# GpSimd builds eight of the twenty-four first one-hots that ScalarE built for the gate tables

## The chip, the cores and the metric

The kernel runs on one core of one Trainium2 chip. The metric is the device time of one execution in microseconds (us); lower is better. Times of the profile count from the first instruction of the profiled execution.

## The reference

The program computes one layer of a decoder for 1024 tokens with 1024 channels. It ends in an expert retrieval (PEER): each token has 8 heads, and each head picks 16 of 128 x 128 experts by two sub-keys, with a softmax over the 16 scores as gates.

```python
idx, gates = peer_retrieve(xf, w_query, sub_keys)     # (T, 8, 16) expert numbers and gates
u, v = expert_u[idx], expert_v[idx]                   # 16384 experts of 1024 numbers
act = gelu(einsum('tkd,td->tk', u, x))                # exact gelu
out = einsum('tk,tkd->td', gates * act, v)
```

The rest of the layer (a pooling mixer and a short convolution mixer, two norms, two projections) lies ahead of the part that this change touches.

## The kernel before

**Two ways through the experts.** The 1024 tokens are eight tiles of 128. Four tiles are *gathered*: GpSimd issues one indirect DMA for each of a tile's 128 (head, choice) pairs, for `expert_u` and again for `expert_v` (1024 in all, into a ring of `RING` = 8 slots), and VectorE multiplies or adds each row. The other four tiles are *dense*: TensorE multiplies their tokens with all 16384 experts, and a table of gates, which is zero wherever an expert was not chosen, weights the result.

**The gate tables.** The table of one token is a 128 x 128 matrix, the sum over its 128 choices of (one-hot of the first half of the expert number) times (gate times one-hot of the second half): one matmul with both one-hots as operands. One dense tile is filled by 128 scattering DMAs of GpSimd (`scatter`), the other three (384 tokens) by these matmuls, in `BATCHES` = 48 batches of `HOTS` = 8 tokens. A batch b passes through four engines:

- VectorE makes the gated one-hots of every batch (eight `TENSOR_SCALAR` of 128 x 128, L1467), and for even b the first one-hots too (one `TENSOR_TENSOR`, L1463).
- ScalarE makes the first one-hots of odd b in `first_hots`: eight `Square` activations (L985), a drain, one `Relu` (L987). It does so two batches ahead: in its loop it calls `first_hots(b + 2)` before it evicts batch b.
- TensorE multiplies (L798): eight matmuls, each shown as two in the profile, in two halves that each fill one PSUM bank of four.
- ScalarE evicts each half (L1009, twice a batch) into one of two stages; SyncE writes a stage to HBM after every fourth batch.

The one-hots have `HOTBUFS` = 3 buffers, so a maker of batch b waits until TensorE is done with batch b - 3 (`table_full`). After batches 5, 13, 21, 29, 37 and 45 (`AFTER_BATCH`) TensorE also multiplies one *score tile* of the dense part (L785, eight matmuls of 512 columns), and ScalarE applies Gelu to it (L993). `pe.wait_ge(hot_first, ...)` holds TensorE at odd b until ScalarE's one-hots are there.

**Around it.** Every engine runs its instructions in the order of the code. GpSimd's queue ahead of the tables holds gathers for two tiles' first rows and the 128 scattering DMAs; `rows` = 64 is the number of gathered rows that VectorE uses before the tables, so GpSimd can issue gathers up to number 71 and then waits (`rows_used`) for VectorE, which comes back to rows after the tables. After the tables TensorE runs the dense part (L785 scores, L831 sums) to the end, and its first sums need gate tables that SyncE reads back from HBM (L557) and VectorE multiplies in (L1252).

Of the kernel before, what the change touches and what calls it, by code (L numbers as in the profile page):

```python
# [9 lines left out]
ACT = mybir.ActivationFunctionType  # L10
AX = mybir.AxisListType

P = 128
# [35 lines left out]
RING = 8  # L49
# [3 lines left out]
HOTS = 8  # L53
HOTBUFS = 3
BATCHES = TABLED * P // HOTS
# [30 lines left out]
def program(nc, hT, x_rows, w_all, sub_keys, pool_w, small, rows_g, expert_u, expert_v, uT, out):  # L86
# [57 lines left out]
    with ctx:  # L144
# [3 lines left out]
        def sem(name):  # L148
            return ctx.enter_context(nc.semaphore(name))
# [31 lines left out]
        hots = at(12288, HOTBUFS * 2 * HOTS, KEYS).rearrange("p (c s t) j -> p c s t j", c=HOTBUFS, s=2)  # L181
        tables = at(18432, STAGES * KEYS, CHUNK).rearrange("p (c j) t -> p c j t", c=STAGES)
        routeT = at(26624, 3, TABLED * P)
# [21 lines left out]
        ones = sb("ones", [P, P])  # L205
        iota = sb("iota", [P, KEYS])
# [88 lines left out]
        d_gates = sem("d_gates")  # L295
        turned = sem("turned")
        turned_out = sem("turned_out")
        hot_first = sem("hot_first")
        hot_gated = sem("hot_gated")
        table_full = sem("table_full")  # L300
        table_out = sem("table_out")
# [55 lines left out]
        rows, since_digits = 0, 0.0  # L357
# [118 lines left out]
        for kind, a, b in order:  # L476
# [19 lines left out]
            elif kind == "sum" and a == GROUPS - 1 and b % 2 == 1:  # L496
                beside[x].append(("dense_root", b // 2))

        block = ctx.enter_context(nc.Block())

        @block.sync
# [126 lines left out]
        @block.gpsimd  # L628
        def _(pool):
            pool.wait_ge(const_dve, 1)  # L630
            nc.gpsimd.affine_select(out=ident[:], in_=ident[:], compare_op=ALU.is_equal, fill=0.0, base=0,
                                    pattern=[[-1, P]], channel_multiplier=1).then_inc(const_pool, 1)
            nc.gpsimd.iota(iota[:], [[1, KEYS]], base=0, channel_multiplier=0,
                           allow_small_or_imprecise_dtypes=True).then_inc(const_pool, 1)
            nc.gpsimd.iota(token_u[:, 0:1], [[0, 1]], base=0, channel_multiplier=1).then_inc(const_pool, 1)
            nc.gpsimd.memset(zeros, 0.0).then_inc(zero_ready, 1)

            head_after = [rows_by[1 if h < 3 else 2] + RING - 1 for h in range(HEADS)]

            def scatter(h):
                if h == 0:
                    pool.wait_ge(zeroed, 16 * ZEROED)
                    pool.wait_ge(s_gates, 1)
                else:
                    pool.wait_ge(scattered, 16 * TOPK * h)
                for k in range(h * TOPK, (h + 1) * TOPK):
                    nc.gpsimd.indirect_dma_start(out=g_flat, out_offset=bass.IndirectOffsetOnAxis(ap=place[:, k:k + 1], axis=0),  # L650
                                                 in_=gate[:, k:k + 1], in_offset=None, compute_op=ALU.add).then_inc(scattered, 16)

            def load_xf(t):
                rank = list(GATHERED_RANK)[t]
                pool.wait_ge(kept[rank % GT], 32 * (rank // GT + 1))
                if t >= 2:
                    pool.wait_ge(rows_used, first_row["u", t - 2] + HK)
                pool.dma_start(xf[:, t % 2, :], of_tile(xf_d, GATHERED_TILE[t])).then_inc(xf_in[t % 2], 16)

            for i, (table, t) in enumerate(ROWS):  # L660
                if table == "u":
                    load_xf(t)
                    if t == 2:

                        pool.wait_ge(routed, GATHERED)
                        pool.dma_start(g_final, rows_g[:, D:2 * D]).then_inc(g_final_in, 16)
                    pool.wait_ge(routed, t + 1)
                else:

                    if t == 0:  # L670
                        pool.wait_ge(keyed, 4 * TILES)
                    else:
                        pool.wait_ge(rows_used, first_row["v", t - 1] + 1)
                    pool.dma_start(h2, of_tile(h2_d, GATHERED_TILE[t])).then_inc(h2_in, 16)
                for k in range(HK):
                    r = HK * i + k
                    if r >= RING:
                        pool.wait_ge(rows_used, r - RING + 1)
                    nc.gpsimd.indirect_dma_start(out=ring[:, r % RING, :], out_offset=None, in_=expert_u if table == "u" else expert_v,  # L679
                                                 in_offset=bass.IndirectOffsetOnAxis(ap=idx[:, t, k:k + 1], axis=0)).then_inc(row_in[r % RING], 16)  # L680
                    for h in range(HEADS):
                        if head_after[h] == r:
                            scatter(h)

        @block.tensor
        def _(pe):
# [15 lines left out]
            for s, (kind, n, i) in enumerate(steps):  # L702
# [3 lines left out]
                if kind == "sumsq":  # L706

                    pe.wait_ge(x_added, n + 1)
                    for k in range(2):
                        last = nc.tensor.matmul(pair[:, 0:width(n)], ones[:], sq[:, k, 0:width(n)], start=(k == 0), stop=(k == 1))  # L710
                elif kind == "pa":
                    if i % 2 == 0:
                        w = next_w()
                    for k in range(KD):
                        if i == 0:
                            pe.wait_ge(xn_ready, KD * n + k + 1)
                        last = nc.tensor.matmul(pair[:, 0:width(n)], w[:, k, i % 2 * P:(i % 2 + 1) * P], xnT[n % 2][:, k, 0:width(n)],  # L717
                                                start=(k == 0), stop=(k == KD - 1))
                elif kind == "bcv":
                    w = next_w()  # L720
                    for c in range(2):
                        last = chunk(pair[:, c * 512:c * 512 + width(n)], w, c, xnT[n % 2][:, :, 0:width(n)])
                elif kind == "pool":
                    if n == 0:
                        pe.wait_ge(const_in, 48)
                    for g in range(NG):
                        pe.wait_ge(pooled, n * NG + g + 1)
                        last = nc.tensor.matmul(pair[:, g * GW:(g + 1) * GW], poolw[:, g, :], yT[:, g, :], start=True, stop=True)
                elif kind == "ynorm":

                    pe.wait_ge(y_added, n + 1)
                    for c in range(2):
                        last = nc.tensor.matmul(pair[:, c * GW:(c + 1) * GW], ones[:], sq[:, c * NG, 0:GW], start=True, stop=True)
                elif kind == "outp":
                    half, t = i // GT, i % GT
# [9 lines left out]
                elif kind == "turn":  # L745
                    pe.wait_ge(xf_ready, n * GT + i + 1)
                    for k in range(KD):
                        last = nc.tensor.transpose(pair[:, k * P:(k + 1) * P], xfb[:, i, k * P:(k + 1) * P], ident[:])
# [13 lines left out]
                elif kind == "score":  # L762
                    if i == 0:
                        pe.wait_ge(act_emptied, empty(("query", n, 3)))
                    t, m = i // 2, i % 2
# [23 lines left out]
            for b in range(BATCHES):  # L789
                c = b % HOTBUFS  # L790
                pe.wait_ge(hot_gated, b + 1)
                if b % 2 == 1:
                    pe.wait_ge(hot_first, b // 2 + 1)
                for m in range(2):
                    if 2 * b + m >= 4:
                        pe.wait_ge(table_out, 2 * b + m - 3)
                    for q in range(4):
                        last = nc.tensor.matmul(g_bank[(2 * b + m) % 4][:, q * KEYS:(q + 1) * KEYS], hots[:, c, 0, 4 * m + q, :],  # L798
                                                hots[:, c, 1, 4 * m + q, :], start=True, stop=True)
                    last.then_inc(table_full, 1)  # L800
                if b == ROUTES_AFTER:
                    pe.wait_ge(d_gates, 2)
                    for t in range(1, TABLED):
                        turn_routes(t)
                if b in AFTER_BATCH:
                    x = AFTER_BATCH.index(b)
                    if x == 0:

                        pe.wait_ge(xfT_in, 16)
                        pe.wait_ge(turned_out, TABLED - 1)  # L810
                    score_tile(x)
# [4 lines left out]
            for kind, a, n in dense:  # L816
# [3 lines left out]
                else:  # L820
                    g, t, half = a, n // 2, n % 2
# [14 lines left out]
        def _(act):  # L836
# [143 lines left out]
            def first_hots(b):  # L980
                c = b % HOTBUFS
                if b >= HOTBUFS:
                    act.wait_ge(table_full, 2 * (b - HOTBUFS) + 2)
                for t in range(HOTS):
                    nc.scalar.activation(hots[:, c, 0, t, :], iota[:], ACT.Square, scale=-1.0, bias=routeT[:, 0, b * HOTS + t:b * HOTS + t + 1])  # L985
                act.drain()
                nc.scalar.activation(hots[:, c, 0], hots[:, c, 0], ACT.Relu, scale=-4.0, bias=ones[:, 0:1]).then_inc(hot_first, 1)  # L987

            def gelu_tile(x):
                if x >= GSLOTS:  # L990
# [7 lines left out]
            for b in range(BATCHES):  # L998
                if b - 1 in AFTER_BATCH:
                    gelu_tile(AFTER_BATCH.index(b - 1))  # L1000
                if b % 2 == 1 and b + 2 < BATCHES:
                    first_hots(b + 2)
                for m in range(2):
                    n = 2 * b + m
                    c, q = n // (CHUNK // 4), n % (CHUNK // 4)
                    if q == 0 and c >= STAGES:
                        act.wait_ge(table_kept[c % STAGES], 16 * (c // STAGES))
                    act.wait_ge(table_full, n + 1)
                    nc.scalar.activation(tables[:, c % STAGES, :, 4 * q:4 * q + 4],  # L1009
                                         g_bank[n % 4].rearrange("p (t j) -> p j t", t=4), ACT.Copy).then_inc(table_out, 1)  # L1010
                if b == ROUTES_AFTER:
                    for t in range(1, TABLED):
                        turn_out(t)
                    act.drain()
# [503 lines left out]
```

## Time and profile before

| | |
|---|---|
| time, median of 3 runs | 2557.34 us (2557.06 to 2560.21) |
| the profiled execution: its time | 2559.86 us |
| its span, first to last instruction | 2558.1 us |
| TensorE busy (matmuls) | 2474.3 us, 97% |
| VectorE busy | 1971.3 us, 77% |
| ScalarE busy | 424.1 us, 17% |
| GpSimd busy | 1452.8 us, 57% |

PE is TensorE's matmuls, PEld its weight loads, DVE VectorE, ACT ScalarE, POOL GpSimd, SP SyncE. "Busy" is a share of the whole span and mixes stages with different limits; the table stage lies between 661 and 822 us.

### The profile page before, as it was taken

How to read it: one execution, taken by the hardware profiler on the slowest of the kernel's cores; microseconds unless marked ns; L12 is line 12 of the kernel's file. 1: busy time of each engine (PE TensorE's matmuls, PEld its weight loads, DVE VectorE, ACT ScalarE, POOL GpSimd, SP SyncE). 2: the span in 40 equal slices, each digit the busy share in tenths (PEclk: the TensorE clock that was granted, in tenths of full speed). 3: DMA queues.
4: the chain of work that ended last, by engine and by line, in shares of the span. 5: the costliest groups of instructions: out<-in, count | busy, mean ns of one | idle time of the engine just before them, and what ended most of it. 6: DMA issues, size and time to landing. Idle time of an engine off the chain costs nothing.

```text
span 2558.1 us, 24120 instructions
## 1 busy us (share of the span) xinstructions
PE 2474.3 (97%) x7561; PEld 1360.4 (53%) x7561; DVE 1971.3 (77%) x4252; ACT 424.1 (17%) x782; POOL 1452.8 (57%) x1169
## 2 busy tenths in 40 slices
PE   8999998998888899999999999999999999999998
PEld 7687785867766344444444444444444444444443
DVE  4308879778779788777898778779787877888877
ACT  0213213221887000110010100000000000000001
POOL 0000487677601267666665767667676776766664
PEclk9999999998999999999999999999999999999999
DMA  8544886865666899989999999999999999999997
GB/s 336 214 156 163 315 300 167 347 188 132 198 190 201 333 356 374 396 318 385 388 413 391 383 385 414 394 418 419 419 386 397 412 394 420 419 407 403 420 401 262
DMA packets 288079, 857.68 MB, mean 335 GB/s; under 512 B 42064, under 2 KB 99408, under 8 KB 273360
## 3 DMA queue, kind: packets, MB, share of 16 engines
q0 software_dynamic: 167184, 541.73, 55.4%
q1 hardware_dynamic: 108416, 289.25, 30.0%
q10 hardware_dynamic: 12352, 25.17, 2.6%
q8 instruction: 60, 0.98, 0.1%
q14 instruction: 67, 0.55, 0.1%
HBM read 807.75 MB, written 48.30 MB: 335 GB/s over the span
## 4 chain that ended last, share of the span: by engine, by line
PE 85%; DVE 6%; ACT 4%; DMA 1%; issue 1%; DVEq 1%; POOL 1%; SPq 1%; ACTq 0%
PE pairs L831 34%; PE pairs L785 33%; PE pairs L699 12%; ACT arena L985 2%; PE pairs L742 1%; PE pairs L717 1%; PE pairs L798 1%; ACT arena L1009 1%; DMA arena<-gate_tables 1%; PE pairs L769 1%; ACT pick_all L864 1%; POOL ring L679 1%; DVE topi L1073 0%; DVE topi L1065 0%; ACT arena L987 0%
## 5 line engine op out<-in xcount | busy, mean ns | idle before, releaser
L679 POOL DMA_INDIRECT ring<-in_expert_u,idx x512 | 660.7, 1290 | 610.7 <-DVE dots L1186 343.5
L831 PE MATMUL pairs<-arena 128*128 128x512 f32 x2048 | 883.4, 593 | 7.0 <-DVE arena L1252 6.3
L785 PE MATMUL pairs<-arena 128*128 128x512 f32 x2048 | 882.5, 592 | 0.0
L679 POOL DMA_INDIRECT ring<-in_expert_v,idx x512 | 574.7, 1122 | 290.2 <-DVE arena L1197 129.9
L1186 DVE CUSTOM_DVE_ANT_0 junk<-ring,xf 128x1024 bf16<-128x1024 f32 x512 | 610.5, 1223 | 157.1 <-DMA ring<-in_expert_u,idx 153.0
L831 PEld LDWEIGHTS pairs<-arena 128*128 128x128 f32 x2048 | 389.6, 190 | 498.4 <-issue 497.5
L785 PEld LDWEIGHTS pairs<-arena 128*128 128x128 f32 x2048 | 388.6, 190 | 486.5 <-issue 486.5
L1197 DVE SCALAR_TENSOR_TENSOR arena<-ring,arena 128x1024 f32<-128x1024 f32 x381 | 471.7, 1284 | 63.8 <-DMA ring<-in_expert_v,idx 62.5
L699 PE MATMUL pairs<-arena 128*128 128x256 f32 (+1 forms) x1792 | 399.7, 386 | 7.2 <-ACT arena L946 4.2
L699 PEld LDWEIGHTS pairs<-arena 128*128 128x128 f32 x1792 | 345.5, 193 | 59.5 <-ACT arena L946 5.1
L993 ACT ACTIVATE arena<-pairs 128x512 f32<-128x512 f32 x128 | 76.4, 597 | 1176.2 <-PE pairs L785 1176.2
L650 POOL DMA_INDIRECT gate_tables<-gate,place x128 | 210.8, 1647 | 57.9 <-issue 38.8
L1197 DVE SCALAR_TENSOR_TENSOR xf<-ring,arena,xf 128x1024 f32<-128x1024 f32 x126 | 154.4, 1282 | 8.8 <-DMA ring<-in_expert_v,idx 8.8
L1252 DVE TENSOR_TENSOR arena<-arena 128x512 f32<-128x512 f32 x128 | 87.6, 688 | 61.2 <-ACT arena L993 48.9
L1258 DVE TENSOR_TENSOR arena<-arena,pairs 128x512 f32<-128x512 f32 x128 | 87.5, 684 | 51.6 <-PE pairs L831 50.9
L1467 DVE TENSOR_SCALAR arena<-iota,arena 128x128 f32<-128x128 f32 x384 | 101.3, 347 | 25.5 <-PE pairs L798 25.5
L742 PE MATMUL pairs<-arena 128*128 128x512 f32 x256 | 114.2, 603 | 5.3 <-DVE arena L1377 5.3
L798 PE MATMUL pairs<-arena 128*128 128x128 f32 x768 | 91.4, 277 | 28.1 <-ACT arena L1009 25.3
L798 PEld LDWEIGHTS pairs<-arena 128*128 128x128 f32 x768 | 88.2, 192 | 34.0 <-issue 30.9
L864 ACT ACTIVATE pick_all<-digit,place 128x256 bf16<-128x256 f32 x128 | 80.4, 723 | 42.0 <-DVE digit L1130 41.7
L742 PEld LDWEIGHTS pairs<-arena 128*128 128x128 f32 x256 | 49.4, 194 | 65.3 <-issue 55.8
L1062 DVE MAX8 tops<-arena 128x8 f32<-128x128 f32 x112 | 24.4, 280 | 61.9 <-ACT arena L961 60.7
(174 smaller groups left out, 1062.1 us busy)
## 6 DMA issues: line engine op xcount, KB each, us to landing
arena<-in_w_all SPq DMA_DIRECT2D x80, 1024.0 KB, 6.1
arena<-in_uT SPq DMA_DIRECT2D x128, 512.0 KB, 6.7
arena<-in_expert_v SPq DMA_DIRECT2D x128, 512.0 KB, 8.8
arena<-gate_tables SPq DMA_DIRECT2D x32, 1024.0 KB, 11.3
gate_tables<-arena SPq DMA_DIRECT2D x11, 2048.0 KB, 9.0
gate_tables<-junk ACTq DMA_DIRECT2D x4, 2048.0 KB, 14.0
ring<-in_expert_u,idx POOLq DMA_INDIRECT x512, 8.9
ring<-in_expert_v,idx POOLq DMA_INDIRECT x512, 8.3
```

The costliest lines, as they stand in the source:

```text
L650: nc.gpsimd.indirect_dma_start(out=g_flat, out_offset=bass.IndirectOffsetOnAxis(ap=place[:, k:k + 1], axis=0), in_=gate[:, k:k + 1], in_of ...
L679: nc.gpsimd.indirect_dma_start(out=ring[:, r % RING, :], out_offset=None, in_=expert_u if table == "u" else expert_v, in_offset=bass.Indir ...
L699: last = nc.tensor.matmul(out_, w[:, k, c * P:(c + 1) * P], xn[:, k, :], start=(k == 0), stop=(k == KD - 1))
L742: last = nc.tensor.matmul(pair[:, q * 512:(q + 1) * 512], yT[:, NG * (1 - half) + k, t * P:(t + 1) * P], w_out[q].rearrange("p k n -> p (k ...
L785: last = nc.tensor.matmul(score_bank[x], uslot[:, x % USLOTS, k * P:(k + 1) * P], xfT[:, k, :], start=(k == 0), stop=(k == KD - 1))
L798: last = nc.tensor.matmul(g_bank[(2 * b + m) % 4][:, q * KEYS:(q + 1) * KEYS], hots[:, c, 0, 4 * m + q, :], hots[:, c, 1, 4 * m + q, :], s ...
L831: last = nc.tensor.matmul(o_bank[n % 4], gated[:, x % GSLOTS, t * P:(t + 1) * P], vrows[:, j, half * 512:(half + 1) * 512], start=(j == 0) ...
L864: last = nc.scalar.activation(pick_hot[:, a], digit[:].rearrange("p h s k -> p k (h s)"), ACT.Square, scale=32.0, bias=place16[:, a:a + 1])
L1186: nc.vector.tensor_tensor_reduce(out=junk[:, r % 2, :], in0=row, in1=xf[:, t % 2, :], scale=1.0, scalar=0.0, op0=ALU.mult, op1=ALU.add, ac ...
L1197: nc.vector.scalar_tensor_tensor(out=to[:, k % 2, :], in0=row, scalar=weight[:, k:k + 1], in1=h2 if k == 0 else to[:, k % 2, :], op0=ALU.m ...
L1252: nc.vector.tensor_tensor(s, s, gtab[a // GJ % 2][:, :, a % GJ, :], ALU.mult).then_inc(w_ready, 1)
L1467: last = nc.vector.tensor_scalar(hots[:, c, 1, t, :], iota[:], routeT[:, 1, k:k + 1], routeT[:, 2, k:k + 1], ALU.is_equal, ALU.mult)
```

## The change

GpSimd makes the first one-hots of batches 5, 11, 17, ... 47 (`BY_POOL`, eight batches), by one `TENSOR_SCALAR` for each token. ScalarE makes those of the other sixteen odd batches (`BY_ACT`), where it is asked for them as before. One semaphore becomes two. All of GpSimd's eight batches stand in its queue ahead of gather number `rows + RING` = 72.

```diff
+        BY_POOL = [b for b in range(BATCHES) if b % 6 == 5]
+        BY_ACT = [b for b in range(BATCHES) if b % 2 == 1 and b % 6 != 5]
@@ gpsimd
+            def first_hots(b):
+                c = b % HOTBUFS
+                pool.wait_ge(table_full, 2 * (b - HOTBUFS) + 2)
+                if b // (P // HOTS) > 0:
+                    pool.wait_ge(turned_out, b // (P // HOTS))
+                for t in range(HOTS):
+                    k = b * HOTS + t
+                    last = nc.gpsimd.tensor_scalar(hots[:, c, 0, t, :], iota[:], routeT[:, 0, k:k + 1], None, ALU.is_equal)
+                last.then_inc(hot_pool, 1)
...
                     r = HK * i + k
+                    if r == rows + RING:
+
+                        for b in BY_POOL:
+                            first_hots(b)
                     if r >= RING:
                         pool.wait_ge(rows_used, r - RING + 1)
@@ tensor
-                if b % 2 == 1:
-                    pe.wait_ge(hot_first, b // 2 + 1)
+                if b in BY_ACT:
+                    pe.wait_ge(hot_act, BY_ACT.index(b) + 1)
+                elif b in BY_POOL:
+                    pe.wait_ge(hot_pool, BY_POOL.index(b) + 1)
@@ scalar
-                nc.scalar.activation(hots[:, c, 0], hots[:, c, 0], ACT.Relu, scale=-4.0, bias=ones[:, 0:1]).then_inc(hot_first, 1)
+                nc.scalar.activation(hots[:, c, 0], hots[:, c, 0], ACT.Relu, scale=-4.0, bias=ones[:, 0:1]).then_inc(hot_act, 1)
...
-                if b % 2 == 1 and b + 2 < BATCHES:
+                if b % 2 == 1 and b + 2 in BY_ACT:
                     first_hots(b + 2)
```

GpSimd's queue before, from the second run of scattering DMAs (L650) past the gathers (L679) to the next tile's:

```order
L679 DMA ring<-in_expert_u,idx 128x1024 x36
L650 DMA gate_tables<-gate,place 8388608x1 x48
L679 DMA ring<-in_expert_u,idx 128x1024 x29
L650 DMA gate_tables<-gate,place 8388608x1 x80
L679 DMA ring<-in_expert_u,idx 128x1024 x63
L658 DMA xf<-xf_scratch 128x1024
```

The same stretch of GpSimd's queue now (the scattering DMAs are L656, the gathers L699, the one-hots L673):

```order
L699 DMA ring<-in_expert_u,idx 128x1024 x36
L656 DMA gate_tables<-gate,place 8388608x1 x48
L699 DMA ring<-in_expert_u,idx 128x1024 x29
L656 DMA gate_tables<-gate,place 8388608x1 x80
L699 DMA ring<-in_expert_u,idx 128x1024 x7
L673 TENSOR_SCALAR arena<-iota,arena 128x128 x64
L699 DMA ring<-in_expert_u,idx 128x1024 x56
L664 DMA xf<-xf_scratch 128x1024
```

The 64 one-hot instructions stand behind all scattering DMAs and behind seven more gathers.

ScalarE's queue before, from the first score tile's Gelu (L993) on; L985 and L987 are the first one-hots of an odd batch, L1009 the evictions, two a batch:

```order
L993 ACTIVATE arena<-pairs 128x512
L1009 ACTIVATE arena<-pairs 128x128x4 x2
L985 ACTIVATE arena<-iota,arena 128x128 x8
L987 ACTIVATE arena<-arena,ones 128x1024
L1009 ACTIVATE arena<-pairs 128x128x4 x4
L985 ACTIVATE arena<-iota,arena 128x128 x8
L987 ACTIVATE arena<-arena,ones 128x1024
L1009 ACTIVATE arena<-pairs 128x128x4 x4
```

The same place in ScalarE's queue now (Gelu L1015, one-hots L1007 and L1009, evictions L1031):

```order
L1015 ACTIVATE arena<-pairs 128x512
L1031 ACTIVATE arena<-pairs 128x128x4 x2
L1007 ACTIVATE arena<-iota,arena 128x128 x8
L1009 ACTIVATE arena<-arena,ones 128x1024
L1031 ACTIVATE arena<-pairs 128x128x4 x8
L1007 ACTIVATE arena<-iota,arena 128x128 x8
L1009 ACTIVATE arena<-arena,ones 128x1024
L1031 ACTIVATE arena<-pairs 128x128x4 x4
```

One group of one-hots in three is gone, here that of batch 11, and eight evictions follow each other. The order of instructions on TensorE, VectorE and SyncE is unchanged.

## Rows read from the trace of the kernel before

**Rows 1.** Windows of three stages: busy us of each engine, clock, DMA, GB/s

```profile
661.00:822.00 161.00, 133.08 (x873) 106.68 (x874) 133.56 (x449) 138.52 (x323) 27.00 (x20) 1.00 0.72 215
822.00:860.00 38.00, 30.96 (x71) 13.34 (x70) 25.04 (x102) 4.09 (x6) 8.04 (x7) 0.94 1.03 388
860.00:2520.00 1660.00, 1660.00 (x3866) 734.79 (x3865) 1339.41 (x1939) 109.58 (x176) 1120.60 (x942) 1.00 0.99 393
```

**Rows 2.** Timeline of PE: start, duration, line, operands, count [idle before <-releaser]

```profile
676.35 2.02 PE L798 MATMUL pairs<-arena 128*128 128x128 f32 x16 [1.01 <-ACT arena L1009]
...
704.65 7.03 PE L785 MATMUL pairs<-arena 128*128 128x512 f32 x16
711.52 5.52 PE L798 MATMUL pairs<-arena 128*128 128x128 f32 x48
718.28 3.81 PE L798 MATMUL pairs<-arena 128*128 128x128 f32 x32 [1.24 <-ACT arena L1009]
...
729.24 2.02 PE L798 MATMUL pairs<-arena 128*128 128x128 f32 x16 [1.67 <-ACT arena L1009]
731.10 7.03 PE L785 MATMUL pairs<-arena 128*128 128x512 f32 x16
```

**Rows 3.** Timeline of ACT, one pair of batches and a Gelu

```profile
719.47 2.44 ACT L985 ACTIVATE arena<-iota,arena 128x128 f32<-128x128 f32 x8
...
723.04 2.04 ACT L1009 ACTIVATE arena<-pairs 128x512 f32<-128x512 f32 x4
724.95 2.44 ACT L985 ACTIVATE arena<-iota,arena 128x128 f32<-128x128 f32 x8
...
738.16 0.60 ACT L993 ACTIVATE arena<-pairs 128x512 f32<-128x512 f32 x1 [3.11 <-PE pairs L785]
```

**Rows 4.** Timeline of DVE in the table stage

```profile
670.12 4.27 DVE L1467 TENSOR_SCALAR arena<-iota,arena 128x128 f32<-128x128 f32 x16
...
713.51 2.14 DVE L1467 TENSOR_SCALAR arena<-iota,arena 128x128 f32<-128x128 f32 x8 [5.30 <-PE pairs L798]
715.56 1.22 DVE L1463 TENSOR_TENSOR arena<-iota,arena 128x1024 f32<-128x1024 f32 x1
716.70 4.19 DVE L1467 TENSOR_SCALAR arena<-iota,arena 128x128 f32<-128x128 f32 x16
720.80 1.22 DVE L1463 TENSOR_TENSOR arena<-iota,arena 128x1024 f32<-128x1024 f32 x1
```

**Rows 5.** Timeline of POOL around the table stage

```profile
679.12 1.56 POOL L650 DMA_INDIRECT gate_tables<-gate,place  x1 [0.30 <-issue]
...
688.56 0.94 POOL L679 DMA_INDIRECT ring<-in_expert_u,idx  x1 [0.30 <-issue]
817.61 1.68 POOL L679 DMA_INDIRECT ring<-in_expert_u,idx  x1 [128.11 <-DVE dots L1186]
```

**Rows 6.** Groups by line on POOL: count | busy, mean ns | idle before

```profile
L636 POOL MEMSET junk<- 128x512 f32 x1 | 0.5, 514 | 0.0
L631 POOL TENSOR_SCALAR_AFFINE_SELECT ident<-ident 128x128 f32<-128x128 f32 x1 | 0.3, 293 | 0.6 <-DVE ident L1048 0.6
L633 POOL IOTA iota<- 128x128 f32 x1 | 0.2, 235 | 0.0
```

**Rows 7.** Timeline of PE after an idle gap

```profile
577.53 9.61 PE L742 MATMUL pairs<-arena 128*128 128x512 f32 x16 [5.07 <-DVE arena L1377]
```

**Rows 8.** Window of that gap: busy us by engine, granted clock, DMA, GB/s

```profile
575.00:580.00 5.00, 2.47 (x3) 1.17 (x4) 3.89 (x4) 0.83 (x3) 3.08 (x3) 0.57 0.15 0
```

**Rows 9.** Groups by shape on DVE: one tile read, and two

```profile
L1195 DVE TENSOR_SCALAR arena<-ring,arena 128x1024 f32<-128x1024 f32 x3 | 2.3, 752 | 0.0
L1238 DVE TENSOR_TENSOR arena<-arena 128x1024 f32<-128x1024 f32 x3 | 3.7, 1225 | 0.3
```

**Rows 10.** Timeline of DVE after the tables

```profile
847.02 2.50 DVE L1252 TENSOR_TENSOR arena<-arena 128x512 f32<-128x512 f32 x4 [2.90 <-DMA arena<-gate_tables]
858.39 2.50 DVE L1252 TENSOR_TENSOR arena<-arena 128x512 f32<-128x512 f32 x4 [8.87 <-DMA arena<-gate_tables]
```

More of the change, by code:

```diff
@@ L297, in program @@
         turned_out = sem("turned_out")
-        hot_first = sem("hot_first")
+        hot_act = sem("hot_act")
+        hot_pool = sem("hot_pool")
         hot_gated = sem("hot_gated")
```

## The prediction

> **What bounds the kernel now.** I read the stages first, by windows [rows 1]. From 860 us to 2520 us TensorE is busy 1660 of 1660 us: the dense part runs at TensorE's own pace, so a delay or a gain ahead of it arrives at the end undiminished, unless the short stage between swallows it. In the table stage (661 to 822) no engine is full: TensorE 133, VectorE 134, ScalarE 139, GpSimd 27 of 161 us. There the limit is a loop between engines, and the timelines tell which.
>
> The pace is best read at the score tiles. They start at 704.65 and 731.10 [rows 2], so eight batches take 26.45 us; the three cycles behind are alike. Between them TensorE waits for ScalarE's evictions (L1009), 1.24 and 1.67 us a time. ScalarE has no such gap: first one-hots of an odd batch and four evictions take 724.95 - 719.47 = 5.48 us, back to back [rows 3]. Its only large wait is 3.11 us for the score tile. VectorE needs 720.80 - 715.56 = 5.24 us for the same two batches and then stands 5.30 us, out of free one-hot buffers [rows 4]. So ScalarE sets the pace, with VectorE only 0.24 us a pair behind. I split VectorE's work: an odd batch takes 715.56 - 713.51 = 2.05 us, an even one 5.24 - 2.05 = 3.19 us.
>
> **What ScalarE loses.** One group of first one-hots is 723.04 - 719.47 = 3.57 us [rows 3]; eight groups are 28.6 us. That is not the gain, because VectorE is right behind. The new cycle, from score tile to score tile, where b is the batch ahead of the tile: the tile (711.52 - 704.65 = 6.87); batch b+1 on TensorE, whose end frees VectorE's next buffer (1.80, a third of 5.52 less the overlap); 0.30 to VectorE; VectorE makes b+4 to b+8, three odd and two even (3 x 2.05 + 2 x 3.19 = 12.53); 0.30 to TensorE; batch b+8 (731.10 - 729.24 = 1.86). The sum is 23.7 us. (The 0.30 is the gap that rows show from one engine's end to the next one's start.) VectorE cannot work through the tile: it is at most three batches ahead. To this comes up to 1.0 us where ScalarE still has first one-hots ahead of the two evictions that TensorE needs; I take half, 24.2 us. The gain is 2.25 us a cycle, and over the five cycles between six score tiles 11.3 us (8.7 to 13.8). Behind the last tile there is only the same short tail.
>
> **What it costs at the start.** This is the term that decides. Batch 5 is the first that waits for GpSimd, and TensorE did it at 676.35 [rows 2]. GpSimd is still in its scattering DMAs then: they end at 680.7, and seven gathers follow, the last at 688.56 for 0.94 us [rows 5]. Only then come the one-hots, from 689.50 + 0.30 = 689.80. The idle stretch that GpSimd has for them, 128.11 us, begins after batch 5 is due. Nothing covers this: VectorE stops after batch 8 and ScalarE after its one-hots of batch 7, both waiting for batch 5's buffers, and the first score tile stands behind batch 5 in TensorE's queue.
>
> The duration of GpSimd's `TENSOR_SCALAR` is in no row. The nearest is the affine select, 128 x 128 in and out, 0.293 us; below it the iota, which reads nothing, 0.235; above it the memset of four times the elements, 0.514 [rows 6]. I take 0.29, as the select reads and writes the same tile size: 8 x 0.29 = 2.3 us (1.9 to 4.1). Batch 5 starts at 689.80 + 2.3 + 0.3 = 692.4, that is 16.1 us late (15.7 to 17.9).
>
> TensorE stands idle some 17 us before it. After an idle gap of 5.07 us, 16 matmuls took 9.61 us where they take 7.03 in a score tile of the same shape, with a granted clock of 0.57 in that window, so near the lower level of 1.2 GHz [rows 7, 8]. I add those 2.6 us (0 to 4).
>
> **Two engines at SBUF at once.** Later one-hots of GpSimd run beside VectorE, which they did not before. Whether they hold each other up no row shows. The lower bound is nothing: with GpSimd issuing DMAs, 16 of VectorE's instructions took 4.27 us, and 4.19 without [rows 4]; but issuing reads no tile. The upper bound is that VectorE stands for every GpSimd instruction: 8 x 0.29 = 2.3 us a batch. Of the seven later batches, 11, 17, 29, 35 and 41 are made while VectorE is on the path above, 23 and 47 while it runs ahead beside the tile: 5 x 2.3 = 11.7 us. I take 7 us of it, since VectorE's `TENSOR_SCALAR` treats 1024 elements in 0.752 us where a two-tile operation takes 1.225 [rows 9]: it seems to move two elements at a time, so it would use more of the memory's ports than it otherwise needs, while some of the standing falls in the half microsecond of slack in the cycle.
>
> The Trainium skill, page "SBUF — State Buffer", section "Who interferes with whom", says that VectorE in a two-port mode, or with two SBUF inputs against a GpSimd instruction that reads, shares one port pair with GpSimd under an exclusive lock, and that the second to come waits for the whole instruction. By that rule the term is the upper bound, and the time would be 2576.4 instead of 2571.7; by the row on DMA issue it would be 2564.7. The trace of before has no GpSimd read beside VectorE, so it decides nothing.
>
> **Sum.** 16.1 + 2.6 - 11.3 + 7 = +14.4 us. Afterwards the score tiles 6 to 9 follow, and the gate tables come back from HBM: VectorE waits 2.90 and 8.87 us for them [rows 10]. That load follows the last eviction, so it moves by the same amount, and nothing is saved there. The profiled execution, 2559.86 us with 2558.1 of span, would become 2574.3; the median of the runs is 2.5 us lower, 2557.34, and becomes **2571.7 us**.
>
> **The rivals.**
> - *No hold-up between GpSimd and VectorE.* The same sum without the 7 us: +7.4, 2564.7 us, and with a shorter one-hot or no slow clock down to about 2561. For it: the 4.27 against 4.19. Against it: it rests on instructions that touch no tile.
> - *GpSimd's one-hots are much slower*, 0.6 us or more, past the memset row. Then batch 5 comes 2.5 us later, VectorE may stand up to 4.8 us a batch, and GpSimd's batch (4.8 us or more) is late for TensorE as well, since it may start only when batch b-3 is done: the gain of 11.3 is gone, and two thirds of 5 x 4.8 = 24 are added: 16.1 + 2.5 + 2.6 + 16 - 11.3 to 0 = +26 to +37, 2583 to 2594 us.
> - *The delay is swallowed* in the 38 us behind the tables, where DMAs are at 1.03 of their capacity [rows 1]: if the queues are emptier when the gate tables are asked for, the 8.87 us wait shrinks by up to as much. Up to 9 us off: about 2561, within the bound below. Against it: the traffic there is issued by the same events, all equally late.
> - *The other side: the cycle falls to VectorE's own work*, 4 x 5.24 = 20.96 us, because VectorE no longer stands beside the score tile. Gain 5 x 5.5 = 27.5, so 16.1 + 2.6 - 27.5 = -8.8: 2548.5 us. It decides at a cycle of 26.45 - 18.7 / 5 = 22.7 us; below that the kernel is faster. Against it: three buffers hold 8.4 us of VectorE's work, while tile and batch b+1 keep them for 6.87 + 1.8 + 0.3 = 9.0, and VectorE must just have finished b when TensorE starts it.
>
> **How the numbers follow.** The forecast has 0.45, no hold-up 0.28, slow one-hots 0.12, swallowed 0.08, the other side 0.07. One measurement of this kernel can tell about 0.2% from no change, 5.1 us: 2552.2 to 2562.5. The forecast lies above for nearly all its terms; of "no hold-up" about a quarter falls within (0.07); swallowed within; the other side mostly below, a little within. That gives faster 0.06, same 0.15, slower 0.79. The range leaves out the other side and most of the slow one-hots: 2559 to 2583.
>
> **What the new profile would show.** TensorE's first L820 matmuls of batch 5 at about 692.4 instead of 676.35, behind a wait of some 16 us that ends with GpSimd's L673; right behind it a granted clock below 1. GpSimd's `TENSOR_SCALAR` near 0.3 us, and start to start more than that where VectorE works. ScalarE then waits for TensorE at its evictions, and VectorE no longer has its 5.3 us a cycle but 1 to 3. Score tiles 24 to 26 us apart. VectorE's `TENSOR_SCALAR` beside GpSimd's longer than its 0.26 us start to start, if they hold each other up; unchanged, if the first rival is right. From 860 + 14 us on everything as before. The prediction is wrong if batch 5 does not wait for GpSimd, if the tiles come closer than 22.7 us, or if the stage behind the tables gives the delay back.

## The result, and the profile after

Over six runs of each kernel on the same chips, the change takes 2575.36 us (2569.45 to 2579.46) and the kernel before 2560.18 us (2557.06 to 2563.72). The ratio is 1.0057, 95% interval 1.0044 to 1.0069: about 14.6 us slower. The forecast was 14.4 us on top of 2557.34 us, so 2571.7 us; the measured median is 3.7 us above that and within the stated range of 2559 to 2583 us.

The page of the profiled execution after, its span and the busy times:

```profile
span 2574.2 us, 24110 instructions
...
PE 2477.0 (96%) x7561; PEld 1364.1 (53%) x7561; DVE 1976.7 (77%) x4252; ACT 399.5 (16%) x710; POOL 1524.7 (59%) x1233
```

ScalarE has 72 instructions fewer and GpSimd 64 more, and ScalarE is 24.6 us less busy. The timeline of GpSimd (start, duration, operands, count, idle before) shows where its new work lies; these answer to [rows 5]:

```profile
690.96 0.94 POOL L699 DMA_INDIRECT ring<-in_expert_u,idx  x1 [0.30 <-issue]
691.93 4.67 POOL L673 TENSOR_SCALAR arena<-iota,arena 128x128 f32<-128x128 f32 x8
713.16 6.22 POOL L673 TENSOR_SCALAR arena<-iota,arena 128x128 f32<-128x128 f32 x8 [16.56 <-PE pairs L820]
733.93 5.60 POOL L673 TENSOR_SCALAR arena<-iota,arena 128x128 f32<-128x128 f32 x8 [14.55 <-PE pairs L820]
...
822.47 5.49 POOL L673 TENSOR_SCALAR arena<-iota,arena 128x128 f32<-128x128 f32 x8 [7.64 <-PE pairs L820]
```

The timeline of TensorE, which answers to [rows 2] (L820 was L798, L805 was L785):

```profile
664.49 2.05 PE L820 MATMUL pairs<-arena 128*128 128x128 f32 x16 [1.17 <-ACT arena L983]
...
696.70 3.76 PE L820 MATMUL pairs<-arena 128*128 128x128 f32 x16 [18.91 <-issue]
700.25 7.45 PE L805 MATMUL pairs<-arena 128*128 128x512 f32 x16
...
739.63 7.45 PE L820 MATMUL pairs<-arena 128*128 128x128 f32 x64 [2.23 <-DVE arena L1489]
...
750.11 7.03 PE L805 MATMUL pairs<-arena 128*128 128x512 f32 x16
...
825.41 7.03 PE L805 MATMUL pairs<-arena 128*128 128x512 f32 x16
```

Batch 5 waits until GpSimd's first eight one-hots end at 691.93 + 4.67 = 696.60. The label "issue" of the 18.91 us names no engine; the two times do. The same reading helps at 739.63: the wait of 2.23 us is put down to VectorE, but VectorE's part of batch 17 ended at 736.20, and GpSimd's at 733.93 + 5.60 = 739.53. It is GpSimd again: TensorE starts batch 17 at 739.63, 0.10 us after GpSimd's part of it is ready. The windows of the change (busy us by engine, granted clock, DMA, GB/s) around batch 5:

```profile
690.00:695.00 5.00, 0.00 (x0) 0.00 (x0) 0.00 (x0) 0.00 (x0) 4.65 (x8) 0.50 0.97 364
695.00:700.00 5.00, 3.30 (x15) 3.33 (x16) 0.00 (x0) 0.60 (x1) 1.60 (x3) 0.50 0.26 107
700.00:705.00 5.00, 5.00 (x14) 2.33 (x13) 3.28 (x9) 1.88 (x2) 0.00 (x0) 0.89 0.00 0
705.00:710.00 5.00, 5.00 (x30) 3.56 (x28) 0.47 (x2) 1.67 (x3) 0.00 (x0) 1.00 0.25 75
```

From 690 to 695 us GpSimd alone works, and TensorE's clock is granted at 0.50, the lower level of 1.2 GHz, until the score tile brings it back.

**The 16.1 us between the two profiled executions** (spans 2574.2 and 2558.1), from TensorE's timelines. Ahead of the tables: the first L820 is at 664.49, L798 was at 662.03, +2.5 us; the code there is the same, and the other kernels below show this point anywhere between 657.4 and 669.4, so I count it as scatter. From there to the first score tile: 35.76 against 16.18, +19.6 us. The five cycles between score tiles: 24.76, 25.10, 25.87, 24.34, 25.09, mean 25.03 against 26.45, -7.1 us. Behind the tables up to the long run of sums: 39.48 against 38.35, +1.1 us. The dense part: the same within 0.1 us.

### The profile page after: what moved, and what is told of

It is laid out like the page before. It is cut to its first block, busy times and chain, and to the rows that moved or that the text cites. A ratio compares the mean times of both kernels' runs of the same rounds, so it can differ in the third digit from the quotient of the medians.

```text
span 2574.2 us, 24110 instructions
## 1 busy us (share of the span) xinstructions
PE 2477.0 (96%) x7561; PEld 1364.1 (53%) x7561; DVE 1976.7 (77%) x4252; ACT 399.5 (16%) x710; POOL 1524.7 (59%) x1233
## 4 chain that ended last, share of the span: by engine, by line
PE 88%; DVE 5%; ACT 2%; DMA 2%; issue 1%; DVEq 1%; SPq 1%; ACTq 0%
PE pairs L853 34%; PE pairs L805 33%; PE pairs L719 15%; PE pairs L820 2%; PE pairs L762 1%; PE pairs L737 1%; DMA arena<-gate_tables 1%; PE pairs L789 1%; DMA arena<-in_w_all 1%; DVE arena L1489 1%; ACT arena L1007 1%; SPq L558 0%; ACT pick_all L886 0%; ACT arena L1031 0%; DVE topi L1095 0%
## 5 line engine op out<-in xcount | busy, mean ns | idle before, releaser
L699 POOL DMA_INDIRECT ring<-in_expert_u,idx x512 | 666.5, 1302 | 489.9 <-DVE dots L1208 224.8
L805 PE MATMUL pairs<-arena 128*128 128x512 f32 x2048 | 883.0, 592 | 0.0
L699 POOL DMA_INDIRECT ring<-in_expert_v,idx x512 | 593.1, 1158 | 267.6 <-DVE arena L1219 121.5
L805 PEld LDWEIGHTS pairs<-arena 128*128 128x128 f32 x2048 | 388.9, 190 | 486.6 <-issue 486.6
L1015 ACT ACTIVATE arena<-pairs 128x512 f32<-128x512 f32 x128 | 76.4, 597 | 1183.6 <-PE pairs L805 1164.1
L656 POOL DMA_INDIRECT gate_tables<-gate,place x128 | 212.7, 1662 | 53.8 <-issue 38.8
L820 PE MATMUL pairs<-arena 128*128 128x128 f32 x768 | 92.5, 280 | 39.1 <-issue 22.8
L820 PEld LDWEIGHTS pairs<-arena 128*128 128x128 f32 x768 | 89.8, 195 | 44.4 <-issue 41.3
L673 POOL TENSOR_SCALAR arena<-iota,arena 128x128 f32<-128x128 f32 x64 | 45.7, 729 | 90.4 <-PE pairs L820 90.4
```

Source lines behind the costliest of these rows:

```text
L805: last = nc.tensor.matmul(score_bank[x], uslot[:, x % USLOTS, k * P:(k + 1) * P], xfT[:, k, :], start=(k == 0), stop=(k == KD - 1))
```

## The experiments

For each kernel the text gives the ratio to the kernel before with its interval, and from its trace the length of the table stage (first table matmul to the first of the four score tiles behind the tables; 158.85 us before, 171.36 us with the change) and the mean cycle between the six score tiles. The stage is the sharper measure: what lies ahead of it scatters by several microseconds.

### ScalarE makes batch 5

```diff
-        BY_POOL = [b for b in range(BATCHES) if b % 6 == 5]
+        BY_POOL = [b for b in range(BATCHES) if b % 6 == 5 and b > 5]
```

> The changed kernel, but ScalarE makes batch 5's first one-hots, so GpSimd has only the seven batches 11, 17, ... 47. Theory (the loss is the place of batch 5 in GpSimd's queue): the 17.9 us wait ahead of batch 5 and the slow clock behind it (2.1 us) vanish, the shorter cycles stay (25.0 instead of 26.45 us, five of them): about 7 us faster than before, ratio near 0.997. Rival (the loss is GpSimd and VectorE holding each other up, or slow one-hots): still slower than before, by 5 us or more.

Measured: ratio 0.9993 (0.9980 to 1.0005). The stage takes 153.32 us, 18.0 us less than in the change and 5.5 less than before; the mean cycle is 25.34 us. The loss is gone with one batch of eight, so batch 5 on GpSimd carries it; the kernels that move batch 5 in the queue, below, show that it is its place. The gain of 7 us over before did not come: the time shows no difference from before (1.8 us by the ratio, and the interval includes none). The cycles are uneven (24.68, 26.72, 25.87, 24.35, 25.09), and 1.5 us are given back behind the tables (39.83 against 38.35 us). The second cycle, with batch 17 on GpSimd, is 1.6 us longer than in the change (25.10), and TensorE's clock is the reason. Its timeline, and a window (busy us by engine, granted clock, DMA, GB/s):

```profile
720.67 9.01 PE L820 MATMUL pairs<-arena 128*128 128x128 f32 x64 [2.22 <-DVE arena L1489]
```

```profile
722.00:724.00 2.00, 2.00 (x12) 2.00 (x11) 1.52 (x4) 1.70 (x3) 0.00 (x0) 0.51 1.02 291
```

The change has the same wait for batch 17 (2.23 us) and the clock at 1.00 behind it, and there the 64 matmuls take 7.45 us. So a late batch can cost more than its wait.

### GpSimd makes only batch 5

```diff
-        BY_POOL = [b for b in range(BATCHES) if b % 6 == 5]
+        BY_POOL = [5]
```

> The kernel before with one batch moved: GpSimd makes only batch 5's first one-hots, behind its scattering DMAs and seven gathers; ScalarE makes all others. Theory (place in the queue): batch 5 starts some 18 us late and TensorE's clock is low behind it, the cycles stay at 26.45 us: 18 to 20 us slower than before, more than the whole change. Rival (hold-up): one batch of GpSimd work costs at most 5 us.

Measured: ratio 1.0057 (1.0043 to 1.0071), stage 178.77 us, 19.9 us longer than before, cycles from the second on 26.44 us as before. The timeline of TensorE (the window ends within the last row):

```profile
671.72 1.95 PE L820 MATMUL pairs<-arena 128*128 128x128 f32 x16
692.58 3.75 PE L820 MATMUL pairs<-arena 128*128 128x128 f32 x16 [18.91 <-issue]
696.13 7.42 PE L805 MATMUL pairs<-arena 128*128 128x512 f32 x16
703.38 1.84 PE L820 MATMUL pairs<-arena 128*128 128x128 f32 x15
```

Eight instructions on GpSimd cost 19.9 us of the stage. By the stage this is 7.4 us more than the whole change costs, as the theory asks; the timed ratio equals that of the change (14.6 us, 11 to 18), short of the 18 to 20 us that I expected, and the two intervals leave room for only part of those 7 us. The profiled execution is the longest of its six (2578.6 us, the others 2574.0 to 2575.7). The profiles and the times agree on the sign and not fully on the size.

### Batch 5 earlier in GpSimd's queue

```diff
                 for k in range(h * TOPK, (h + 1) * TOPK):
+                    if k == HK - 4:
+                        first_hots(5)
...
-                        for b in BY_POOL:
+                        for b in BY_POOL[1:]:
```

> The changed kernel with one move: batch 5's one-hots stand ahead of GpSimd's last four scattering DMAs instead of behind all of them and seven gathers. The same work on each engine. Theory (place): batch 5 starts within 2 us of before; GpSimd reaches batch 11 some 5 us later than without batch 5, which may cost up to 3 us once; 3 to 7 us faster than before. Rival (the GpSimd work itself costs): 5 us or more slower than before, like the change.

Measured: ratio 1.0006 (0.9992 to 1.0019); stage 158.22 us, 13.1 us less than with the change, with the same instructions on every engine. The first score tile comes 15.11 us into the stage, earlier than before (16.18). But the first cycle takes 30.65 us, 6.0 us more than that of the kernel with batch 5 on ScalarE (24.68), where I had allowed up to 3 us. GpSimd starts batch 11 16.6 us behind the score tile, there 12.5 us. TensorE's wait for it, and a window behind:

```profile
706.87 8.48 PE L822 MATMUL pairs<-arena 128*128 128x128 f32 x48 [3.97 <-DVE arena L1491]
```

```profile
708.00:710.00 2.00, 2.00 (x12) 2.00 (x11) 0.92 (x4) 0.60 (x1) 0.00 (x0) 0.50 1.15 348
```

GpSimd's batch ended at 706.77, so it is again what TensorE waited for. Of the 6.0 us some 2.9 are the lower clock behind the wait: three batches in a row take 8.48 us, in the other kernel 5.60. Why batch 11 started late is open: GpSimd's last gather ends at 700.06, but the trace has it wait for TensorE until 701.16. The profiled execution is also the slowest of its twelve, 7.9 us above their median. So the direction held against the change, and the expected 3 to 7 us over before did not come.

### Batch 5 behind the scattering DMAs, ahead of the seven gathers

```diff
+                    if r == rows + 1:
+                        first_hots(5)
                     if r == rows + RING:
...
-                        for b in BY_POOL:
+                        for b in BY_POOL[1:]:
```

> The changed kernel, with batch 5's one-hots directly behind the scattering DMAs and ahead of the seven gathers, the rest as in the change. Seven gathers take 8.7 us of queue, so by the theory of the place batch 5 starts about 9 us late instead of 18 and the table stage is about 9 us shorter than in the change: 3 to 6 us slower than before. If the place does not matter, like the change, 14 us slower.

Measured: ratio 1.0039 (1.0026 to 1.0053). The first score tile comes 26.89 us into the stage, 8.9 us sooner than with the change (35.76), which is about the queue time of seven gathers. The stage is 164.86 us, 6.5 us shorter. The rest went to the granted clock: the first cycle is 0.8 us longer than in the change because the first score tile takes 8.11 us instead of 7.29, and the second 1.5 us longer (26.63 against 25.10) because the 64 matmuls behind the wait for batch 17 take 8.98 us instead of 7.45, with the clock at 0.51. By the ratio the kernel is 10 us slower than before, more than the 3 to 6 us that I expected. Dose and answer go together: with batch 5 on ScalarE the first score tile comes after 16.2 us, behind the scattering DMAs after 26.9, behind these and the gathers after 35.8.

### Nobody makes seven batches

```diff
-        BY_POOL = [b for b in range(BATCHES) if b % 6 == 5]
+        BY_POOL = []
+        BY_NONE = [b for b in range(BATCHES) if b % 6 == 5 and b > 5]
```

> Leaves out work: nobody makes the first one-hots of batches 11, 17, ... 47 (the matmuls read what the buffer held), ScalarE makes all others, batch 5 too. What is left is the cycle without any GpSimd work. By the path of the prediction, 24.2 us a cycle (23.7 to 24.7): 9 to 14 us faster than before. The distance to the kernel in which GpSimd makes those seven batches is the whole cost of GpSimd's slowness and of the hold-up: 7 us if the prediction's term was right, near 0 if they do not disturb each other.

Measured: ratio 0.9973 (0.9956 to 0.9989), stage 150.37 us. The cycles are 26.02, 24.53, 24.54, 24.11 and 24.54 us, mean 24.75. The first holds a wait of ScalarE, at the eviction of batch 8, for a table stage to be written out; the others average 24.43 us. My path had 24.2. So without any GpSimd work the five cycles gain 8.5 us, 10.1 without that one wait, where I had 11.3; the time is 6.9 us shorter than before, not the 9 to 14 us that I expected. Timeline of ScalarE in the first cycle:

```profile
692.36 1.06 ACT L1032 ACTIVATE arena<-pairs 128x512 f32<-128x512 f32 x2
695.67 2.56 ACT L1032 ACTIVATE arena<-pairs 128x512 f32<-128x512 f32 x5 [2.25 <-DMA gate_tables<-arena]
```

No other kernel waits at this eviction; those that wait for a write early on do so some 10 us later in the stage (1.3 us before, 3.3 to 3.8 us in the three kernels that follow, around a score tile). Why the write ended later here is not known.

### The same GpSimd work into a spare tile

```diff
-                    last = nc.gpsimd.tensor_scalar(hots[:, c, 0, t, :], iota[:], routeT[:, 0, k:k + 1], None, ALU.is_equal)
+                    last = nc.gpsimd.tensor_scalar(spare[:, t * KEYS:(t + 1) * KEYS], iota[:], routeT[:, 0, k:k + 1], None, ALU.is_equal)
```

> Leaves out the first one-hots of batches 11, 17, ... 47 like the kernel in which nobody makes them, but GpSimd makes the same 56 one-hots at the same points into a spare tile that nobody reads, so TensorE never waits for GpSimd. What it differs by from the kernel with nobody is the pure hold-up at SBUF: 5 x 2.3 us or more if VectorE stood for every instruction (a cycle of 27 us), near 0 (24.8 us) if lateness was the cost. VectorE's instructions beside GpSimd's show it directly.

The kernel has waits more than the change: GpSimd waits for its own batch before, and VectorE's later rows and a load of SyncE wait until the spare tile is free.

Measured: ratio 0.9970 (0.9961 to 0.9980), stage 148.94 us, cycles 24.35, 24.54, 24.54, 24.35, 24.54, mean 24.46. That is as long as with nobody, without that one wait (24.43). Its timelines of GpSimd and of VectorE (L1496 are the gated one-hots):

```profile
709.84 5.62 POOL L678 TENSOR_SCALAR junk<-iota,arena 128x128 f32<-128x128 f32 x8 [14.55 <-PE pairs L825]
723.00 5.52 POOL L678 TENSOR_SCALAR junk<-iota,arena 128x128 f32<-128x128 f32 x8 [7.54 <-PE pairs L825]
```

```profile
709.78 2.33 DVE L1496 TENSOR_SCALAR arena<-iota,arena 128x128 f32<-128x128 f32 x8 [2.37 <-PE pairs L825]
...
713.17 4.44 DVE L1496 TENSOR_SCALAR arena<-iota,arena 128x128 f32<-128x128 f32 x16
...
718.66 4.19 DVE L1496 TENSOR_SCALAR arena<-iota,arena 128x128 f32<-128x128 f32 x16
...
723.91 4.70 DVE L1496 TENSOR_SCALAR arena<-iota,arena 128x128 f32<-128x128 f32 x16
```

Beside GpSimd VectorE's 16 instructions take 4.44 and 4.70 us, and 4.19 without. A GpSimd batch holds VectorE up by 0.4 to 0.5 us here, and by up to 1.0 us elsewhere, not by the 5.5 to 6.4 us of its own length. The cycle has room for it, since it is as long with nobody.

### Half of each batch

```diff
-                for t in range(HOTS):
+                for t in range(HOTS // 2):
```

in GpSimd's `first_hots`, with ScalarE making batch 5.

> The kernel in which ScalarE makes batch 5 and GpSimd batches 11, 17, ... 47, but GpSimd makes only four of each batch's eight first one-hots (the other four are left out), so its batches take half as long. Theory (GpSimd's batches are late, since each starts only when the batch three before is done and takes 5.5 to 6.4 us): with half of the work it is never late, and the cycle falls from 25.3 to about 24.8 us, that of the kernel in which nobody makes them. Rival (hold-up of VectorE): half of the difference stays, 25.05 us.

Measured: ratio 0.9966 (0.9955 to 0.9978), stage 148.44 us, cycles 24.10, 24.54, 24.54, 24.11, 24.53, mean 24.36. The cycles of 25.9 and 26.7 us have vanished. Together with the spare tile this settles what GpSimd's later batches cost: not the hold-up, but that a batch may start only when the one three before it is done and then takes 5.5 to 6.4 us, so TensorE waits for it at some places of the cycle, and now and then runs at the lower clock behind the wait. Which places, the cycles tell: 25.9 us is the cycle with batch 29, 25.1 us those with batches 17 and 41 (26.6 to 26.7 where the clock fell behind batch 17), while the fourth cycle, with batch 35, takes 24.3 to 24.4 us in every kernel in which GpSimd makes all of it.

### One batch in eight, at one place of the cycle

```diff
-        BY_POOL = [b for b in range(BATCHES) if b % 6 == 5]
+        BY_POOL = [b for b in range(BATCHES) if b % 8 == 3 and b > 3]
```

> GpSimd makes the first one-hots of batches 11, 19, 27, 35 and 43, one in each cycle between two score tiles and always the same one; ScalarE makes all others, batch 5 too. These are the batches with which the cycle was shortest (24.3 and 24.7 us against 25.9 and 26.7 with others). Theory: every cycle is near 24.4 us, five of them give 10 us, of which 1.5 us are given back behind the tables: about 8 us faster than before, though GpSimd makes fewer batches than in the kernel with seven. Rival (the gain is the number of batches taken from ScalarE): 5/7 of the gain of the kernel with seven, 4 us or less.

Measured: ratio 0.9974 (0.9962 to 0.9986), about 7 us faster than before. The stage takes 148.37 us, 10.5 less than before, with cycles of 24.36, 24.35, 24.35, 24.35 and 24.35 us. Behind the tables 1.9 us are given back (40.21 against 38.35), and 0.9 more in the first sums (120 matmuls in 54.22 us against 53.34), which leaves 7.7 us. Its timeline of TensorE, one cycle (the window ends within the last row):

```profile
697.96 7.03 PE L805 MATMUL pairs<-arena 128*128 128x512 f32 x16
704.83 5.52 PE L820 MATMUL pairs<-arena 128*128 128x128 f32 x48
711.58 3.81 PE L820 MATMUL pairs<-arena 128*128 128x128 f32 x32 [1.24 <-ACT arena L1031]
716.78 5.69 PE L820 MATMUL pairs<-arena 128*128 128x128 f32 x48 [1.39 <-issue]
722.31 1.88 PE L805 MATMUL pairs<-arena 128*128 128x512 f32 x4
```

In the same cycle GpSimd and VectorE:

```profile
710.45 6.23 POOL L673 TENSOR_SCALAR arena<-iota,arena 128x128 f32<-128x128 f32 x8 [18.12 <-PE pairs L820]
```

```profile
710.00 5.11 DVE L1489 TENSOR_SCALAR arena<-iota,arena 128x128 f32<-128x128 f32 x16
...
716.13 4.24 DVE L1489 TENSOR_SCALAR arena<-iota,arena 128x128 f32<-128x128 f32 x16
```

GpSimd is late here too: it ends batch 19 at 716.68, and TensorE, which waited 1.39 us, starts it at 716.78. But VectorE ends batch 21 only at 716.13 + 4.24 = 720.37, and TensorE starts that at 722.31 - 1.86 = 720.45, so the wait for batch 19 is covered. Five batches at the right place gain what seven at mixed places do not. This kernel computes the whole layer and beats both.

## Why the prediction was right, and where it was off

**The start.** The step held: batch 5 behind the scattering DMAs and seven gathers, and nothing to cover it. The forecast was 16.1 us; measured from the first table matmul to batch 5 it is (696.70 - 664.49) - (676.35 - 662.03) = 17.9 us. The 1.8 us are GpSimd's instruction, 2.3 us longer for eight (4.67 us, 0.58 each, where I took 0.29 from the affine select [rows 6]), less 0.5 us by which it began earlier and TensorE followed faster than I took. My upper bound, 0.51 from the memset, was too low as well. The kernels with batch 5 on ScalarE and with only batch 5 on GpSimd show the term by itself. VectorE stopped one batch sooner than I wrote, after batch 7 (18.37 us of waiting ahead of batch 8), which changes nothing in the sum.

**The clock.** Forecast 2.6 us, measured 2.1: batch 5 took 700.25 - 696.70 = 3.55 us against 1.86, and the score tile 7.29 against 6.87.

**The shorter cycle.** The path score tile, batch b+1, five batches of VectorE, was right in kind and a little short: 24.2 us forecast, 24.43 measured with nobody (24.75 with the one wait for a write). What I sized too small is ScalarE's first one-hots ahead of the evictions: half a microsecond on top of 23.7, where 0.8 came, and with nobody TensorE's last waits ahead of the score tiles are for evictions (1.16 and 1.67 us). The five cycles can gain 10 us instead of 11.3.

**Two engines at SBUF.** This term was wrong in size and in kind. I took 7 us for VectorE being held up. The spare tile shows a hold-up of 0.4 to 1.0 us a batch that costs nothing: it lies on VectorE's path, as in the kernel with one batch in eight, but without it ScalarE's evictions keep the cycle as long. What there is, is lateness of GpSimd's batches: the five cycles of the change are 2.8 us longer than with the spare tile (25.03 against 24.46 each), of which 0.4 is the slow clock in the first score tile. The rule of the Trainium skill, page "SBUF — State Buffer", section "Who interferes with whom", by which the second to come waits for the whole instruction, would have made it 11.7 us at my price of a one-hot. This case's traces do not agree: VectorE lost 0.4 to 1.0 us a batch, and GpSimd was the one that got longer, from 4.67 us alone to 5.5 to 6.4; VectorE's `TENSOR_TENSOR`, which has two SBUF inputs, took 1.21 us beside GpSimd (at 717.70) as without. Whether VectorE's `TENSOR_SCALAR` ran in the two-port mode that the rule speaks of, no run shows.

**The sum.** Errors of opposite sign met. Against my terms the start cost 1.8 us more and the clock 0.5 less, the cycles gained 9.9 us (26.45 to the 24.46 of the spare tile) instead of 11.3, so 1.4 too little, and the disturbance cost 2.4 us instead of 7: 14.4 + 1.8 - 0.5 + 1.4 - 4.6 = 12.5 us, which is what the stage shows (171.36 - 158.85). 1.1 us came behind the tables, which I had put at nothing. The term that decides, the start, was right; that the total came within a microsecond is in part luck.

**The rivals.** "No hold-up" was right that the hold-up costs nothing, but not in the time, since lateness took its place. That lateness is what "slow one-hots" described, a batch that may start only when batch b-3 is done and is late for TensorE; its condition was nearly met (0.58 alone, up to 0.80 beside VectorE, against 0.6), but not its price: it let lateness take up to the whole gain of 11.3 us and added two thirds of a full hold-up, where lateness took 2.4 us and the hold-up nothing. "Swallowed" fell: the stage behind the tables took 1.1 us more, not less. The other side fell too: the shortest mean cycle with any kernel was 24.35 us, above the 22.7 below which the change would have been faster.

**Left open.** Every kernel with shorter cycles loses 1.1 to 1.9 us behind the tables, where the second load of gate tables comes back later. Timeline of VectorE in the change, which answers to [rows 10]:

```profile
861.91 2.50 DVE L1274 TENSOR_TENSOR arena<-arena 128x512 f32<-128x512 f32 x4 [0.43 <-DMA arena<-gate_tables]
874.49 2.50 DVE L1274 TENSOR_TENSOR arena<-arena 128x512 f32<-128x512 f32 x4 [10.08 <-DMA arena<-gate_tables]
```

The first wait is 2.5 us shorter than before and the second 1.2 us longer. VectorE leaves the tables 7 to 8 us ahead of that point instead of 10, so its gathers fall differently among the loads; no run tells whether that is the cause. Nor was tried what makes the time ahead of the tables scatter, nor why TensorE's clock fell behind the 2.2 us wait for batch 17 in three kernels and not in the change.

## What to carry to other kernels

An idle stretch on an engine is of use only from where it begins in that engine's queue. Before work is moved there, compare the time at which the queue reaches the new place with the time at which the first consumer needs it; here the average of 27 us busy in a stage of 161 looked free, and one batch of eight came 18 us too late and cost more than the other seven gained. And which batches are moved matters more than how many: five at the place in the cycle where lateness is covered shortened the stage by 10.5 us and the run by 7, seven at mixed places shortened the stage by 5.5 and the run by nothing that the times can tell.

## What was not expected of the hardware

- GpSimd's `TENSOR_SCALAR` of 128 x 128 with a scalar for each partition takes 0.58 us alone (4.67 us for eight), twice the affine select of the same size (0.293 us), and 0.69 to 0.80 us beside VectorE.
- GpSimd reading SBUF and VectorE in back-to-back `TENSOR_SCALAR` and `TENSOR_TENSOR` slow each other only a little on VectorE's side: 16 `TENSOR_SCALAR` 4.2 to 5.1 us instead of 4.19, one `TENSOR_TENSOR` 1.21 us with and without.
- After 19 us without a matmul, the granted clock was 0.50 in the two windows up to 700 us, and 16 matmuls of 128 columns took 3.55 us instead of 1.86.
- A short wait can be followed by the lower clock too: behind 2.2 us of waiting for batch 17 it was 0.50 to 0.51 in three kernels (with batch 5 on ScalarE, in the middle of the scattering DMAs, and ahead of the gathers), which cost 1.5 to 1.6 us, and 1.00 in the change.
